# Decoder layer with product-key experts: second maxima in PSUM, four banks for the query heads, four expert blocks inside the heads, the last head decoded on VectorE, and the gathered rows one step earlier

## The reference

```python
q = (hf @ w_query).reshape(n, 8, 2, 128)                 # n = 1024 tokens, 8 heads, 2 halves
scores = einsum('nhpd,hpkd->nhpk', q, sub_keys)          # 128 keys per half
s_top, i_top = lax.top_k(scores, 16)
cand_s = s_top[:, :, 0, :, None] + s_top[:, :, 1, None, :]
cand_i = i_top[:, :, 0, :, None] * 128 + i_top[:, :, 1, None, :]
best_s, best_pos = lax.top_k(cand_s.reshape(n, 8, 256), 16)
idx = take_along_axis(cand_i.reshape(n, 8, 256), best_pos)
gates = softmax(best_s)
act = gelu(einsum('thkd,td->thk', expert_u[idx], h))     # 16384 experts of one neuron
out = einsum('thk,thkd->td', gates * act, expert_v[idx])
```

## Time and profile before

| what | us |
|---|---|
| median of 3 runs | 3298.59 (3298.26 to 3298.93) |
| the profiled execution | 3296.84 |
| its span, first to last instruction | 3295.1 |
| PE busy in the span | 3047.8 (92%) |
| DVE busy | 2593.9 (79%) |
| POOL busy | 1266.2 (38%) |
| ACT busy | 1096.8 (33%) |

### The profile page before, as it was taken

The page is one execution under the profiler, slowest core; times in us unless marked ns, Lnnn a source line. Parts: engine busy times, 40 slices in busy tenths (PEclk is TensorE's granted clock), DMA queues, the critical chain, the costliest instruction groups (busy, mean ns, idle before and its releaser), DMA issues. The chain is left out here.

```text
span 3295.1 us, 53113 instructions
## 1 busy us (share of the span) xinstructions
PE 3047.8 (92%) x18277; PEld 2702.7 (82%) x18277; DVE 2593.9 (79%) x5152; ACT 1096.8 (33%) x2021; POOL 1266.2 (38%) x969
## 2 busy tenths in 40 slices
PE   6999999899787779979999999999999999999992
PEld 4998888789666679878888889888888888898882
DVE  5464333464489979959999999999999999999998
ACT  4222666403244445522222222222222222222221
POOL 0001000010177510015555556555555555555553
PEclk9999999999898889989999999999999999999996
DMA  6435333242200018889889889988998988898886
GB/s 238 153 135 167 103 103 106 80 165 79 84 26 14 20 64 255 267 270 323 315 323 320 317 314 325 319 315 320 318 320 314 329 317 316 313 324 323 314 300 234
DMA packets 331871, 760.99 MB, mean 231 GB/s; under 512 B 20348, under 2 KB 171480, under 8 KB 331744
## 3 DMA queue, kind: packets, MB, share of 16 engines
q0 software_dynamic: 115712, 419.48, 35.2%
q1 hardware_dynamic: 214976, 335.65, 30.9%
q10 hardware_dynamic: 1056, 4.19, 0.3%
HBM read 686.86 MB, written 72.39 MB: 230 GB/s over the span
## 5 line engine op out<-in xcount | busy, mean ns | idle before, releaser
L1940 POOL DMA_INDIRECT ex_u_row<-in_expert_u,ex_row x384 | 487.3, 1269 | 702.5 <-DVE ex_dot L2161 385.9
L1940 POOL DMA_INDIRECT ex_v_row<-in_expert_v,ex_row x384 | 531.0, 1383 | 334.4 <-DVE acc L2174 264.7
L2174 DVE SCALAR_TENSOR_TENSOR acc<-ex_v_row,ex_coef,acc 128x1024 f32<-128x1024 f32 x384 | 491.5, 1280 | 17.1 <-DMA ex_v_row<-in_expert_v,ex_row 3.6
L2161 DVE CUSTOM_DVE_ANT_0 ex_u_row<-ex_u_row,h_rows 128x1024 f32<-128x1024 f32 x384 | 467.3, 1217 | 0.0
L1998 PE MATMUL psum<-ex_v_hi,ex_c_lo 128*128 128x512 f32 x1280 | 422.5, 411 | 34.6 <-DVE acc L2209 24.5
L1998 PE MATMUL psum<-ex_v_lo,ex_c_hi 128*128 128x512 f32 x1280 | 400.2, 394 | 0.0
L1998 PE MATMUL psum<-ex_v_hi,ex_c_hi 128*128 128x512 f32 x1280 | 397.0, 391 | 0.0
L1991 PE MATMUL psum<-h_hi,h_lo 128*128 128x320 f32 x1792 | 300.1, 310 | 5.2 <-DVE h_lo L2151 5.2
L2209 DVE TENSOR_TENSOR acc<-psum,acc 128x512 f32<-128x512 f32 x384 | 263.8, 687 | 51.2 <-PE psum L1998 40.3
L1991 PE MATMUL psum<-h_lo,h_hi 128*128 128x320 f32 x1792 | 300.2, 310 | 0.0
L1991 PE MATMUL psum<-h_hi 128*128 128x320 f32 x1792 | 299.8, 309 | 0.0
(11 more groups left out here) (314 smaller groups left out, 5373.3 us busy)
## 6 DMA issues: line engine op xcount, KB each, us to landing
ex_vn<-in_expert_v SPq DMA_DIRECT2D x64, 1024.0 KB
ex_un<-in_expert_u SPq DMA_DIRECT2D x48, 1024.0 KB
w_dram<-sc_w SPq DMA_DIRECT2D x10, 4096.0 KB, 14.9
ex_w<-w_dram SPq DMA_DIRECT2D x64, 640.0 KB
gm_wm<-in_w_mod SPq DMA_DIRECT2D x16, 1024.0 KB, 5.3
pj_raw<-in_w_in SPq DMA_DIRECT2D x11, 1024.0 KB, 8.4
qk_dram<-pj_staged_r POOLq DMA_DIRECT2D x32, 256.0 KB, 2.6
gt_raw<-in_w_in SPq DMA_DIRECT2D x16, 512.0 KB, 3.7
```

The lines of the kernel that those rows point to most:

```text
L1940: nc.gpsimd.indirect_dma_start(to[:], None, all_rows, bass.IndirectOffsetOnAxis(row[s][:, col:col + 1], 0)).then_inc(done, 16)
L2161: nc.vector.tensor_tensor_reduce(out=u_row[k % 3][:], in0=u_row[k % 3][:], in1=h_rows[:, k % 3, :], scale=1.0, scalar=0.0, op0=ALU.mult, o ...
L2174: nc.vector.scalar_tensor_tensor(out=to, in0=v_row[k % 3][:], scalar=coef[:, k:k + 1], in1=to, op0=ALU.mult, op1=ALU.add).then_inc(row_use ...
```

## The change

- The second half's maxima (`rt_top`, half 1) go to bank 6 of PSUM; the first half's stay in SBUF.
- The query units use banks 0 and 1 in turn for banks 0 to 3, the scores banks 4 and 5 for 4 to 7, and there is one query buffer in place of two.
- The first four jobs (now `HEADS = 4`) are done within heads 4 to 7, their parts set between the units and copies of the head. They use banks 2, 3 and 7, and one buffer of their own for the turned block.
- ScalarE runs `one_hot` of head d - 2 in the middle of `chunk(d)`, behind the first half's scores; before, it ran ahead of the chunk.
- SP loads the first two blocks ahead of the weights of heads 4 to 7.
- The last head is located and its one-hots multiplied by VectorE straight after its rank, ahead of `conclude(6)`, in 2-byte elements laid out in pairs, and folded by halving additions.
- Experts: the four GELUs of step 0 come before ScalarE waits for the stores of the scatter stage, and the turning and splitting of step 1 follow them. All dots and additions of rows are done one step earlier; six of each go from the end of the loop to its start.

```diff
-        self.turn_bank, self.hide_bank = core.bank[0:2], core.bank[2:4]
+    def place_heads(self):
+        at = self.core.at
+        self.un = [at(f"ah_un_rt{m}", 136 + 4 * m, [P, D]) for m in range(2)]
+        self.ut_hi, self.ut_lo = ([at(f"ah_{n}", kb, [P, KD, P], F32R)[:]] * 2 for n, kb in (("hi", 88), ("lo", 92)))
+        self.turn_bank, self.hide_bank = self.core.bank[2:4], (self.core.bank[7], self.core.bank[2])
...
-    top = core.at("rt_top", 196, [P, TT, 2, TOPK])
+    top = (core.at("rt_top", 197.25, [P, TT, TOPK])[:], core.bank[6][:, 0:TT * TOPK].rearrange("p (t k) -> p t k", k=TOPK))
...
+            def units(d, half, j):
+                ring.channels_unit(nc, pe, core.bank[j % 2], d % 2, j % 2, h, half, d * U + j)
...
+            for d in range(PH):
+                n = d - FIRST_JOB
+                job = 0 <= n < JOBS
+                ring.ready(pe, d % 2, d // 2)
+                units(d, 0, 0)
+                if job:
+                    ahead.turn(pe, n, n % 2, n // 2)
+                units(d, 0, 1)
+                scores(d, 0)
+                if job:
+                    ahead.leave(pe, n, n % 2)
+                units(d, 1, 2)
+                if job:
+                    ahead.hide(pe, n, n % 2, 0)
+                units(d, 1, 3)
+                if job:
+                    ahead.hide(pe, n, n % 2, 1)
+                scores(d, 1)
...
+            def chunk(d, exps=None):
+                n = d - FIRST_JOB
+                job = 0 <= n < JOBS
+                if d + 1 < PH:
+                    ring.split_hi(nc, act, (d + 1) % 2, (d + 1) // 2, d * U)
+                queries(d, 0)
+                if job:
+                    ahead.upper(act, n, n % 2)
+                queries(d, 1)
+                score(d, 0)
+                if job:
+                    ahead.lower(act, n, n % 2)
+                if exps is not None:
+                    one_hot(exps)
+                queries(d, 2)
+                queries(d, 3)
+                score(d, 1)
+                if job:
+                    for half in range(2):
+                        ahead.gelu(act, n, half, first=n == 0)
+            chunk(0)
+            chunk(1)
+            for h in range(PH - 2):
+                exponentials(h)
+                chunk(h + 2, h)
+            exponentials(PH - 2)
+            one_hot(PH - 2)
...
+            def pick_last():
+                for p in range(2):
+                    nc.vector.tensor_tensor(last_hot[:, p], last_ab[:, p].unsqueeze(2).to_broadcast([P, HB, TOPK, 2]),
+                                            last_iota[:].unsqueeze(1).to_broadcast([P, HB, TOPK, 2]), ALU.is_equal)
...
             for h in range(1, PH):
                 search(h, h % 2)
                 combine(h)
+                if h == LAST:
+                    locate_last(LAST % 2)
+                    pick_last()
                 conclude(h - 1)
-            locate(1)
-            conclude_last(LAST, 1)
+            conclude_last(LAST)
...
-            weigh(0, 0, 0)
+            for k in range(3):
+                row_dot(0, k)
+                dve.drain().then_inc(row_used, 1)
             for q in range(4):
                 split_u(0, 1, q, q)
+            weigh(0, 0, 0, first=True)
             split_v(0)
-            weigh(0, 1, 0, dots=0)
+            for k in range(3):
+                row_dot(0, 3 + k)
+                row_add(0, k)
+            weigh(0, 1, 0, dots=1, adds=0)
...
-                weigh(i, j + 2, i * (PERIOD // 2) + (j // 2 + 1), dots=c + 1, adds=c)
+                weigh(i, j + 2, i * (PERIOD // 2) + (j // 2 + 1), dots=c + 2, adds=c + 1)
...
             for k in range(3):
-                row_dot(NSTEP - 1, k)
-                row_add(NSTEP - 2, 3 + k)
-            add(NI, PERIOD - 1, False)
-            for k in range(3):
                 row_add(NSTEP - 1, 3 + k)
+            add(NI, PERIOD - 1, False, True)
```

More of the change, by code:

```diff
@@ L1217 @@
 class Ahead:
-    TAIL = 4
+    HEADS = 4
     BLOCKS = NKEYS // 8
@@ L1343, in _ @@
             ahead.load(sp, 1, 1)
+            for d in range(4, PH):
+                query_weights(d)
             for n in range(JOBS):
@@ L1407, in _ @@
                 last.then_inc(sk_turned, 1)
[L1408 to L1423, removed]
+            ahead.prime_tensor(pe)
@@ new lines, in units, with scores @@
+            def units(d, half, j):
+                ring.channels_unit(nc, pe, core.bank[j % 2], d % 2, j % 2, h, half, d * U + j)
+            def scores(h, half):
+                pe.wait_ge(q_copied, h * U + 2 * half + 2)
+                for m in range(2 * half, 2 * half + 2):
+                    pe.wait_ge(sc_copied, 4 + h * U + m - 1)
+                    for k in range(4):
+                        tt, p = 2 * m + k // 2, k % 2
+                        last = nc.tensor.matmul(core.bank[4 + m % 2][:, k * P:(k + 1) * P], q[:, p, tt * P:(tt + 1) * P],
+                                                sk_t[:, 2 * h + p, :], start=True, stop=True)
+                    last.then_inc(scored, 1)
@@ L1435, in _ @@
                 last.then_inc(h_turned, 1)
[L1436 to L1442, removed]
-                        (ahead.leave if half else ahead.turn)(pe, n + 1, (n + 1) % 2, *(() if half else ((n + 1) // 2,)))
-                    ahead.hide(pe, n, n % 2, half)
         @block.scalar
@@ L1524, in _ @@
+            exponentials(PH - 1)
         @block.vector
@@ L2175, in row_add, with weigh @@
                                                op0=ALU.mult, op1=ALU.add).then_inc(row_used, 1)
-            def weigh(i, j, use, dots=None, adds=None):
+            def weigh(i, j, use, dots=None, adds=None, first=False):
                 c, s = i * PERIOD + j, j % 2
@@ L2183, in weigh @@
                     to = slice(half * HD, (half + 1) * HD)
-                    flat = act_out[n % 2][:] if n < units(j) else pre[:, half, :]
+                    flat = act_out[n % 2][:] if n < units(j) and (n < 2 or not first) else pre[:, half, :]
                     x = flat.rearrange("p (b t) -> p b t", t=t.WB)
@@ L2197, in weigh, with add @@
                                             ALU.subtract).then_inc(c_lo, 1)
-                    if n < rows:
-                        if adds is not None:
-                            row_add(adds, 3 + n)
-                        elif dots is not None:
-                            dve.drain().then_inc(row_used, 1)
-            def add(i, j, turning=True):
+                    if adds is not None and n < rows:
+                        row_add(adds, 3 + n)
+            def add(i, j, turning=True, last=False):
                 c = i * PERIOD + j
+                r = c + 1
                 for n in range(NU):
@@ L2391, in decoder_layer @@
         core.end_early()
-        ahead.place("sc", 180, 197)
+        ahead.place_scatter()
         t.WB = 64
```

227 lines of the change are left out of this document (117 added, 110 removed).

## The result

The changed kernel takes 3260.60 us (median of 4 runs, 3259.64 to 3263.84), the kernel before 3298.43: a ratio of 0.9888 (95% interval 0.9873 to 0.9902), 37.8 us faster. The forecast was 3264, so 35 us faster. The profiled execution took 3260.53 us, with a span of 3258.8 (before 3295.1).

The account below looks back on a forecast made before the run. VectorE was taken to bound the heads, TensorE the expert loop. Savings of 17.0 (heads), 16.8 (last head) and 1.2 (rows), 35.0 us in all, took 3298.59 to 3264 us, range 3255 to 3277.

Parts of the forecast that it names:

- Second maxima in PSUM: Heads: freed sums, with the new bank and job order, start search 7 at 1115.5 for 1132.51, 17.0 us less.
- The mechanism and the price: Heads: sums with one PSUM input stop waiting for GpSimd, 5.3 us in heads 2 to 5; small PSUM instructions cost zero.
- absorb most of it, so I add nothing: Heads 4 and 5: concluding additions meet weight splits, up to 3.7 us each; 2.5 us score waits mostly cover it.
- I add 1.5 us: Heads: correction for slow score matmuls on TensorE after two idles ahead of head 4, 1.5 us.
- the ring: Heads: TensorE starts the next head only after one-hots, GpSimd's last product and weight split; 31.0 us, under 32.3, not binding.
- Last head: Retrieval tail: decoding the last head at once takes 16.4 us after the rank in place of 33.2, 16.8 less.
- Rows one step earlier: Expert stage: the end gains 8.9 us, the start costs 7.7, together 1.2 us less.
- 62 steps cost the same: Expert loop: same instructions in the same order with indices one higher, so no change in its time.
- since TensorE is further ahead: Expert stage start: TensorE's lead takes 0.7 us off VectorE's time from weights tile to first addition.
- the weights tile is not delayed: Rival, expert stage start: gathers come late or fit gaps, so 7.5 us less, 3256.5 us; chance 0.14.
- My estimate: Heads: the skill's dearer PSUM fixed cost, 65 ns for each of 40 small instructions, or 2.6 us a head.
- the maxima with one input do not wait: Heads: VectorE's one-input maxima took 273 to 297 ns, whatever GpSimd did.

Follow-up runs that it names:

- e1: Changed kernel with the second maxima back in SBUF, all else as changed: 3285.4 us, 0.9967 of the kernel before.
- e5: Kernel before with only the second maxima moved to PSUM, the scores giving up two of their four banks: 3285.1 us, ratio 0.9965.
- e2: Changed kernel with a head's concluding additions moved behind the first maxima of the next search but one: 3265.4 us, 0.9906 of the kernel before.
- e7: Changed kernel with the expert stage of the kernel before (rows not shifted, GELUs of step 0 behind the store wait): 3264.7 us, 0.9901 of the kernel before.
- e4: Changed kernel with GpSimd holding the second set of early gathers until the first routing-weights tile has landed: 3259.6 us, 0.9885 of the kernel before.
- e9: Changed kernel with the last head decoded as in the kernel before, all else as changed: 3267.9 us, 0.9913 of the kernel before.
- e6: Kernel before with only the decoding of the last head changed, jobs still in the tail: 3297.7 us, ratio 1.0001.

## Why the prediction was right, and where it was not

The marks of the two profiled executions give 36.3 us where the forecast had 35.0. That it is so close is partly luck: the heads gave 3.0 us less than their term and the expert stage 3.9 more.

**Second maxima in PSUM, 17.0 predicted, 14.0 measured.** The mechanism and the price hold, and e1, e5 and the rows of the maxima show both. Of the two corrections, "absorb most of it, so I add nothing" was right (e2). The mis-sized term is the other one, "I add 1.5 us" for the low clock. I had scaled it from a wait before the short score matmuls, but the idle stands before the long units of heads 3 and 4. Five kernels have the same order of work in the heads on TensorE, ScalarE and GpSimd, and in all of them the two sums take 0.29 and 0.61 us. In each I take the time from the first unit's start to the next instruction's in heads 3 and 4 (changed: 942.85 to 950.02, 975.69 to 984.12) and subtract twice 5.54, what it takes at full clock (e7, head 3, which has no row at the low level):

| kernel | excess, heads 3 + 4 | search 1 to 7 | difference |
|---|---|---|---|
| changed | 4.52 | 205.98 | 201.46 |
| e2 | 4.46 | 205.88 | 201.42 |
| e4 | 5.29 | 206.72 | 201.43 |
| e7 | 1.65 | 203.09 | 201.44 |
| e9 | 1.57 | 203.00 | 201.43 |

The right column is constant within 0.04 us: the low clock after the two idles is all that separates these executions in the heads, and 4.5 - 1.5 is the 3.0 us that I missed. TensorE started head 3 at 942.85 (predicted 942.8), head 4 at 975.7 (973.8); 1.6 of those 1.9 us are the excess in head 3, so the ring itself took 31.2 us for my 31.0 (its four terms add to 30.5, where I wrote 30.6). The idle is 3.6 us in all ten cases, yet what follows it costs from nothing to 2.9 us. Such a difference can account for a part of the spread of the times; with one trace for each kernel that is not shown, and the expert stage has a spread of its own (1879.4 to 1883.0).

**Last head, 16.8 predicted, 17.0 measured**, pass by pass. The prediction put the whole sum under the decoding, though it did say that the waits go because ScalarE has no jobs; e6 and e9 show that some 11 us of it hang on that.

**Rows one step earlier, 1.2 predicted, 4.6 to 5.1 measured.** Up to the first addition the start costs 8.5 us (7.7 predicted), with a tile 7.0 us late (7.5 predicted); from the first addition of step 62 to the end the kernel gains 10.0 (8.9 predicted). The step that failed is that the loop's "62 steps cost the same": from first addition to first addition they take 1746.2 us for 1749.8. All but 0.1 us of it lies in the first two: 27.5 us for 30.1 and 25.7 for 26.7. From the third on, the loop takes 1693 us in both kernels. It goes with a lead of TensorE, for which I had credited 0.7 us "since TensorE is further ahead". Before VectorE's first addition it had begun two shares in the kernel before (1460.73, 1462.49) and four in the changed one (1427.66, 1430.44, 1432.99, 1437.11). The rows point to the early GELUs, the other part of the change in this stage. The first GELU of step 0 and TensorE's first share, before and changed:

```profile
1429.10 0.44 ACT L2089 ACTIVATE ex_g<-psum 128x320 f32<-128x320 f32 x1 [16.19 <-DMA w_dram<-sc_w]
1460.73 0.62 PE L1998 MATMUL psum<-ex_v_hi,ex_c_lo 128*128 128x512 f32 x2
...
1386.81 0.44 ACT L2132 ACTIVATE ex_g<-psum 128x320 f32<-128x320 f32 x1 [5.07 <-PE psum L2038]
1427.66 0.72 PE L2045 MATMUL psum<-ex_v_hi,ex_c_lo 128*128 128x512 f32 x2 [3.03 <-ACT ex_g L2143]
```

Counted from the clearing, the GELU comes 11 us earlier and the share 1.9 us earlier (49.2 for 51.1), although the tile is 7.0 us later; in the kernel before TensorE waited 4.66 us, from 1432.1 to 1436.8, for the release by these GELUs. TensorE's last share ends 4.3 us later after the clearing than before (1840.3 for 1836.0). e4 shows the same slack from the other side: a tile 7.0 us earlier is worth about 1 us, so the rival "the weights tile is not delayed" was priced far too high at 7.5. How the gain divides between the early GELUs and the shifted rows stays open, since e7 puts back both.

The Trainium skill (VectorE: DVE Perf Modes, the section on the TRN2 errata) gives its dearer fixed cost for a PSUM source, an estimate of 65 ns more. My estimate charged it for all 40 small instructions, though the 16 maxima only write to PSUM. For the 24 loads, which do read it, the trace disagrees, with 4 ns; L873, with its 0.07 us more, is close to the figure. The Trainium skill (SBUF — State Buffer, the section Who interferes with whom) says that a VectorE instruction with two SBUF inputs and a GpSimd instruction that reads SBUF share a port pair, which the first to start holds for its whole length while the other blocks fully; e1 agrees, with each sum getting through within 0.5 us of the end of an instruction of GpSimd.

## What to carry to other kernels

Where one engine's instruction is stretched by another's, moving an operand to PSUM is worth what the order of work makes it collide with: 13 us in one order, 24 in another; and an order that is slower by itself can be free after it. Parts of a change can depend on each other so much (the same decoding of the last head gave nothing on the kernel before and 5.8 us on the changed one) that each has to be tried on both kernels. An idle of a few microseconds on TensorE can cost more than itself, when the long matmuls behind it run at the low clock (0 to 2.9 us here behind 3.6 us of idle): look for the ring that makes the idle, here a weight split queued behind products that wait for ScalarE.

## What the runs showed that I had not expected

An instruction of VectorE with one SBUF input can wait as well. In e6 a cast of 128 elements took 4.13 us (its row above), where the like one takes 0.22 in the changed kernel; it ended at 1164.24, and GpSimd's two products ran from 1156.02 to 1164.15, the first of them to 1160.10. The shift of 128 elements ahead of it took 0.76 us for 0.23 and ended at 1160.18. My prediction's "the maxima with one input do not wait" holds for maxima, not for these two. The Trainium skill (SBUF — State Buffer, the section Who interferes with whom) names instructions in a two-port mode beside those with two SBUF inputs; the row agrees with it if the cast runs in such a mode, which no run here shows.
